# A hybrid decoder step on one core: the first expert step placed after the second group's combine, and the sample's attention on 128 rows

## The reference, cut to what matters

```
q, k, v, u = x @ w_in
a = diff_attention(q, k, v)          # 4 heads, two maps each: softmax0 - lam * softmax1, ALiBi, causal
s = s5_mixer(u)                      # state space branch
x = layer_norm(ALPHA * x + concat(a, s) @ w_out)
x = layer_norm(ALPHA * x + peer(x))

def diff_attention(...):             # sample: q 8 x 8 rows, k and v: 8 cached pages of 128 rows, and the 8 new rows
    s = einsum('bqhcd,bkhcd->bhcqk', q, k) * DQK ** -0.5
    s = where(causal, s - slope[h] * abs(dist), MASK)
    p = softmax(s)
    o = einsum('bhqk,bkhd->bqhd', p[:, :, 0] - lam * p[:, :, 1], v)
    return rms_norm(o, subln_g) * (1 - lam_init)

def peer(x):                         # 8 heads, 16 of 16384 single-neuron experts for each head and row
    q = rms_norm(x @ w_q)
    s_top, i_top = top_k(q @ sub_keys, 16)           # two halves of 128 keys
    best, pos = top_k(all 256 sums of a pair of halves, 16)
    g = softmax(best)
    act = gelu(einsum('thkd,td->thk', u_tab[idx], x))
    return einsum('thk,thkd->td', g * act, v_tab[idx])
```

## Time and profile before

| | us |
|---|---|
| median of 3 runs | 3920.2 |
| lowest, highest | 3915.3, 3923.3 |
| the profiled execution's own time | 3909.7 |
| its span, first to last instruction | 3907.1 |
| busy in the span: PE, DVE, ACT, POOL | 2720.8, 2430.5, 1499.2, 1285.4 |
| first gather, last gather issued at | 483.1, 3882.9 |
| mean granted clock of TensorE | 0.781 |

### The profile page before, as it was taken

How to read it: one execution, slowest core, us unless ns; L and a number is a source line. 1 busy time by engine, 2 the same in 40 slices (tenths; PEclk the granted TensorE clock), 3 DMA queues, 4 the chain that set the end, 5 groups by cost and what they waited for, 6 DMA issues and landing times.

```text
span 3907.1 us, 43487 instructions
## 1 busy us (share of the span) xinstructions
PE 2720.8 (70%) x13628; PEld 1104.0 (28%) x13628; DVE 2430.5 (62%) x5666; ACT 1499.2 (38%) x4347; POOL 1285.4 (33%) x1099
## 2 busy tenths in 40 slices
PE   7999475666676666666766776667666767787666
PEld 4677221122122212221232223123212332232221
DVE  8501486568557855775577558766876685334684
ACT  1111134434444444434443444344445444333343
POOL 0000034433443344344434442444344332112333
PEclk9999777786777678777877777678767877888866
DMA  6321499989999999899989998999899989767888
GB/s 140 82 81 57 152 404 398 413 333 384 402 379 371 371 405 369 360 382 417 375 341 395 410 370 339 397 410 379 343 397 411 372 342 378 268 253 302 326 341 344
DMA packets 240485, 1308.09 MB, mean 335 GB/s; under 512 B 41618, under 2 KB 69554, under 8 KB 90482
## 3 DMA queue, kind: packets, MB, share of 16 engines
q0 software_dynamic: 156672, 1140.92, 72.6%
q1 hardware_dynamic: 81890, 159.13, 11.8%
q10 hardware_dynamic: 1696, 5.27, 0.4%
HBM read 1285.65 MB, written 17.97 MB: 334 GB/s over the span
## 4 chain that ended last, share of the span: by engine, by line
DMA 30%; DVE 22%; PE 19%; ACT 8%; issue 7%; POOL 2%; SPq 2%; DVEq 0%; POOLq 0%
DMA UV<-in_peer_uv,icur 29%; DVE junk L1380 9%; PE psum L1045 9%; PE psum L971 3%; PE psum L991 3%; POOL UV L880 2%; PE psum L949 2%; ACT L1145 2%; ACT D L1150 1%; ACT wge L1147 1%; DMA wq<-in_cache_k 1%; DVE E L1340 1%; DVE sc L1287 1%; DVE E L1347 1%; ACT E L1056 1%
## 5 line engine op out<-in xcount | busy, mean ns | idle before, releaser
L1045 PE MATMUL psum<-UV,D 64*64 64x512 f32 x8704 | 1557.0, 810 | 1030.7 <-ACT D L1150 945.8
L880 POOL DMA_INDIRECT UV<-in_peer_uv,icur x1088 | 1279.8, 1176 | 2217.4 <-PE psum L1045 1788.7
L1380 DVE CUSTOM_DVE_ANT_0 junk<-UV,x 128x1024 bf16<-128x1024 f32 x1088 | 1333.7, 1226 | 862.1 <-DMA UV<-in_peer_uv,icur 791.9
L1145 ACT ACTIVATE ge<-acts 128x1 f32<-128x1 f32 x1088 | 219.7, 202 | 1774.0 <-DVE acts L1380 1772.9
L1045 PEld LDWEIGHTS psum<-UV,D 64*64 64x64 f32 x8704 | 321.7, 163 | 1953.3 <-issue 1860.6
L1150 ACT ACTIVATE D<-id,wge 128x64 f32<-128x64 f32 x1088 | 378.3, 348 | 35.4
L1147 ACT ACTIVATE wge<-ge,gcur 128x1 f32<-128x1 f32 x1088 | 320.5, 295 | 35.3
L991 PE MATMUL psum<-wq,aT 128*128 128x256 f32 (+1 forms) x1152 | 307.3, 426 | 1.2 <-ACT aT L1095 1.2
L991 PEld LDWEIGHTS psum<-wq,aT 128*128 128x128 f32 (+1 forms) x1152 | 235.2, 210 | 118.8 <-issue 72.4
L1145 ACT ACT_TABLE_LOAD x112 | 143.7, 1283 | 2.0
L308 PE MATMUL psum<-w_in_sb,xT 128*128 128x256 f32 (+1 forms) x576 | 129.6, 383 | 0.0
(11 more groups left out here) (295 smaller groups left out, 2415.4 us busy)
## 6 DMA issues: line engine op xcount, KB each, us to landing
wq<-in_peer_w_q SPq DMA_DIRECT2D x72, 1024.0 KB, 9.1
UV<-in_peer_uv,icur POOLq DMA_INDIRECT x1088, 10.1
wq<-in_cache_k SPq DMA_DIRECT2D x64, 256.0 KB, 7.1
vrows<-in_cache_v SPq DMA_DIRECT2D x64, 256.0 KB, 6.6
w_in_sb<-in_w_in SPq DMA_DIRECT2D x8, 1024.0 KB, 7.2
x<-in_x_all SPq DMA_DIRECT2D x9, 512.0 KB, 14.5
w_out_sb<-in_w_out SPq DMA_DIRECT2D x1, 4096.0 KB, 17.3
out<-x ACTq DMA_DIRECT2D x8, 512.0 KB, 7.1
```

Source lines behind the costliest of these rows:

```text
L880: pool.indirect_dma_start(out=UV[:, n % RING, :], out_offset=None, in_=table, in_offset=bass.IndirectOffsetOnAxis(ap=icur[:, t % 2, column ...
L1045: ins = pe.matmul(bank[6 + r][q:q + 64, :], D[64 * r:64 * r + 64, n % RING, :], UV[64 * r:64 * r + 64, n % RING, DM + 512 * e:DM + 512 * e ...
L1145: act.activation(ge[:, j:j + 1], acts[:, j:j + 1], ACT.Gelu).then_inc(sem("gelu_done"), 1)
L1380: dve.tensor_tensor_reduce(out=junk[:, :], in0=UV[:, n % RING, 0:DM], in1=x1[:, t % 2, :], scale=1.0, scalar=0.0, op0=ALU.mult, op1=ALU.ad ...
```

## The change

`lead(t)` is now five steps past the start of the combine of group 1 instead of group 0: 88 for a prompt tile and 96 for the sample tile. The first expert step of a tile so follows the second group's combine. Since index copies of several groups of the sample tile can now be under way before its first gather, the semaphore `spread` is split into one for each group.

The sample's attention uses 128 rows, 32 for each head (of which 16 are used: two maps of eight queries). A score matmul of a head writes its own 32 PSUM rows, with no adding over heads, and a value matmul of a head takes only this head's 128 columns of V. The map is transposed with all 128 rows, in two PSUM banks and two copies. The head mask `wm` goes; four scalings write the diagonal blocks of `Om`, a part of `E` that is set to zero once.

```diff
         def lead(t):
 
-            return combine_at(t, 0) + 5
+            return combine_at(t, 1) + 5
...
             if t == NT:
-                wait(pool, "spread", 16 + 32 * (g + 1))
+                wait(pool, f"spread{g}", 32 if g else 48)
...
                 for h in range(H):
-                    last = pe.matmul(bank[e][0:64, 0:n], qbd[:, h, :], kT[:, h, k0:k0 + n], start=h == 0, stop=h == H - 1)
+                    last = pe.matmul(bank[e][32 * h:32 * h + 32, 0:n], qbd[:, h, :], kT[:, h, k0:k0 + n], start=True, stop=True)
...
             for pg in range(PG):
-                pe.transpose(bank[0][:, 64 * pg:64 * pg + 64], Ef[0:64, P * pg:P * pg + P], ident[0:64, 0:64])
+                pe.transpose(bank[pg // 4][:, pg % 4 * P:(pg % 4 + 1) * P], Ef[:, P * pg:P * pg + P], ident[:, :])
...
             for pg in range(PG):
-                pe.matmul(bank[2][0:64, :], aT[:, pg, 0:64], vrows[:, pg, :], start=pg == 0, stop=False)
-            pe.matmul(bank[2][0:64, :], PTn[:, :], vnew, start=False, stop=True).then_inc(sem("s_O"), 1)
+                for h in range(H):
+                    pe.matmul(bank[2][32 * h:32 * h + 32, 0:DV], aT[:, pg, 32 * h:32 * h + 32], vrows[:, pg, h * DV:(h + 1) * DV],
+                              start=pg == 0, stop=False)
+            for h in range(H):
+                last = pe.matmul(bank[2][32 * h:32 * h + 32, 0:DV], PTn[:, 32 * h:32 * h + 32], vnew[:, h * DV:(h + 1) * DV],
+                                 start=False, stop=True)
+            last.then_inc(sem("s_O"), 1)
...
-                act.activation(aT[:, :, 0:64], bank[0][:, :].rearrange("p (g r) -> p g r", g=PG), ACT.Copy)
-                act.activation(PTn[:, :], bank[1][0:DS, 0:64], ACT.Copy).then_inc(sem("s_PT"), 1)
+                for e in range(2):
+                    act.activation(aT[:, 4 * e:4 * e + 4, :].rearrange("p g r -> p (g r)"), bank[e][:, :], ACT.Copy)
+                act.activation(PTn[:, :], bank[2][0:DS, 0:P], ACT.Copy).then_inc(sem("s_PT"), 1)
...
                 for c in range(2):
-                    for h in range(H):
-                        last = dve.tensor_copy(flat[64 * c:64 * c + 64, 80 * h + DS * c:80 * h + DS * c + DS],
-                                               qT[64 * c:64 * c + 64, h, DS * b:DS * b + DS])
+                    last = dve.tensor_copy(qbd[64 * c:64 * c + 64, :, DS * c:DS * c + DS],
+                                           qT[64 * c:64 * c + 64, :, DS * b:DS * b + DS])
...
                 wait(dve, "s_O", b)
-                dve.tensor_tensor(Ef[0:64, SEQ + 16:SEQ + 16 + DA].rearrange("p (h v) -> p h v", h=H),
-                                  bank[2][0:64, :].rearrange("p (h v) -> p h v", h=H),
-                                  wm[:, 0:H].rearrange("p (h u) -> p h u", u=1).broadcast_to((64, H, DV)), ALU.mult)\
-                   .then_inc(sem("s_Om"), 1)
+                for h in range(H):
+                    last = dve.tensor_scalar(Om[32 * h:32 * h + 32, h * DV:(h + 1) * DV], bank[2][32 * h:32 * h + 32, 0:DV],
+                                             small[32 * h:32 * h + 32, 6:7], None, ALU.mult)
+                last.then_inc(sem("s_Om"), 1)
```

More of the change, by code:

```diff
@@ L766, in trunk @@
         Ef = E[:, :]
+        Om = E[:, SEQ + 16:SEQ + 16 + DA]
         def S2(c, nk):
@@ L864, in sp_spread @@
                 wait(sp, "x1_ready", NT + 1)
-                sp.dma_start(x1[SR:P, NT % 2, :], x1[0:SR, NT % 2, :]).then_inc(sem("spread"), 16)
+                sp.dma_start(x1[SR:P, NT % 2, :], x1[0:SR, NT % 2, :]).then_inc(sem("spread0"), 16)
             p0, p1 = groups(NT)[g]
@@ L869, in sp_spread @@
                 pairs = cur[:, NT % 2, TOP * p0:TOP * p1].rearrange("p (q s k) -> p s q k", s=2, k=TOP)
-                sp.dma_start(pairs[SR:P, 0, :, :], pairs[0:SR, 1, :, :]).then_inc(sem("spread"), 16)
+                sp.dma_start(pairs[SR:P, 0, :, :], pairs[0:SR, 1, :, :]).then_inc(sem(f"spread{g}"), 16)
         def pool_gather(pool, t, k):
@@ L1188, in dve_sample_setup @@
             wait(dve, "aT_ps", 4 * NT)
-            step(dve.tensor_scalar(bias[0:64, 0:WB], bias[0:64, 0:WB], rowc[:, 6:7], None, ALU.add))
-            step(dve.tensor_scalar(bias[0:64, WB:SEQ], bias[0:64, WB - P:WB], float(P), None, ALU.add))
-            step(dve.tensor_scalar(bias[0:64, SEQ:], iot[0:64, 0:DS], rowc[:, 0:1], None, ALU.subtract))
-            step(dve.tensor_scalar(wm[:, 0:DS], bias[0:64, SEQ:], 0.0, MASKED, ALU.is_gt, ALU.mult))
-            step(dve.tensor_tensor(bias[0:64, SEQ:], bias[0:64, SEQ:], wm[:, 0:DS], ALU.add))
+            step(dve.tensor_scalar(bias[:, 0:WB], bias[:, 0:WB], rowc[:, 6:7], None, ALU.add))
+            step(dve.tensor_scalar(bias[:, WB:SEQ], bias[:, WB - P:WB], float(P), None, ALU.add))
+            step(dve.tensor_scalar(bias[:, SEQ:], iot[:, 0:DS], rowc[:, 0:1], None, ALU.subtract))
+            step(dve.tensor_scalar(wm[:, 0:DS], bias[:, SEQ:], 0.0, MASKED, ALU.is_gt, ALU.mult))
+            step(dve.tensor_tensor(bias[:, SEQ:], bias[:, SEQ:], wm[:, 0:DS], ALU.add))
+            step(dve.memset(Om, 0.0))
         def dve_sample(dve, step, b, r):
@@ L1501, in _ @@
                 q, slope, mw, hf, cf, rf = (rowc[:, n:n + 1] for n in range(6))
+                spare = rowc[:, 7:8]
                 step(dve.tensor_copy(rf, rowi[:, 0:1]))
-                for dst, sh, mask in ((q, 0, DS - 1), (cf, 3, 1), (hf, 4, H - 1)):
+                for dst, sh, mask in ((q, 0, DS - 1), (cf, 3, 1), (hf, 5, H - 1), (spare, 4, 1)):
                     step(dve.tensor_scalar(rowi[:, 1:2], rowi[:, 0:1], sh, mask, ALU.arith_shift_right, ALU.bitwise_and))
@@ L1508, in _ @@
                 step(dve.tensor_scalar(rowc[:, 6:7], rowc[:, 6:7], float(SEQ - P - PAST), None, ALU.add))
-                step(dve.tensor_scalar(mw, neglam[0:64, :], -1.0, None, ALU.add))
+                step(dve.tensor_scalar(mw, neglam[:, :], -1.0, None, ALU.add))
                 step(dve.tensor_scalar(mw, mw, cf, 1.0, ALU.mult, ALU.add))
-                step(dve.tensor_scalar(headm[:, :], iot[0:64, 0:H], hf, None, ALU.is_equal))
+                step(dve.tensor_scalar(headm[:, :], iot[:, 0:H], hf, None, ALU.is_equal))
                 step(dve.tensor_scalar(slope, headm[:, 0:1], SLOPE[0], None, ALU.mult))
@@ L1519, in _ @@
                 step(dve.memset(sel[:, :], 0.0))
-                step(dve.tensor_scalar(sel[:, 56:56 + DS], iot[0:64, 0:DS], q, None, ALU.is_equal))
+                step(dve.tensor_scalar(spare, spare, 64.0, None, ALU.mult))
+                step(dve.tensor_tensor(spare, spare, q, ALU.add))
+                step(dve.tensor_scalar(sel[:, 56:56 + DS], iot[:, 0:DS], spare, None, ALU.is_equal))
                 for f in range(lead(0)):
```

38 lines of the change are left out of this document (18 added, 20 removed).

## The result

| | before | after |
|---|---|---|
| median, us | 3921.3 (4 runs) | 3803.2 (4 runs) |
| lowest, highest | 3915.3, 3923.3 | 3797.1, 3809.7 |
| ratio, 95% interval | | 0.9701 [0.9682, 0.9721] |
| span of the profiled execution | 3907.1 | 3795.2 |

The change takes 118 us off, 109 to 125 by the interval. The forecast was 3800 us, 120 us less than before.

A forecast was written before the change was run, and what follows sets the result against it. DMA was taken as the bound, with time to win only where its engines are not full. Boundaries -77, last boundary -16, startup +7 and sample -34 make -120 us, giving 3800 us as likeliest, range 3760 to 3848.

The forecast's parts named there:

- The seven boundaries: Tile boundaries before the last: gathers no longer wait for group 0's combine, 11 of 12.9 us saved each, -77 us in all.
- VectorE's deficit: Around a tile boundary VectorE falls 6 us behind DMA; buffers cover most, not TensorE's stall for the sum; 2 us idle left.
- The last boundary: Boundary into the sample tile, where group 1 waits for its spread too: -16 us of 22.1, bounds -10 to -20.
- The start: Tile 0: nothing hides front steps 78 to 87, first dot near 501; +7 us, bounds +3 to +12.
- The sample: Sample's attention in tile 7: shorter values save 4.3 us a group, map costs 0.7, last scores save 5; -34 us in all.
- The map's dearer copies: Sample's attention: map transposed in 128 rows and copied by two ScalarE operations instead of one, +0.7 us in the chain.
- DMA moves the same bytes, gathers a little earlier: Sample's attention: the transferred bytes stay the same and gathers come slightly earlier; no time was assigned to this.
- The four heads' scalings: Sample's attention: four scalings of 128 replace one of 512; all VectorE edits cancel within 0.5 us, none in the loop.
- A: Sample's attention: column groups run one after another, values stay 9 to 10 us, sample costs 0 to +12; 3840 us, chance 0.14.
- B: Tile boundaries not freed: combine, sum and layer norm meet, 5 instead of 11 us saved at each of seven; 3842 us, chance 0.15.
- C: Sample's attention: each column-group change costs a drain, 0.28 us a record, deciding from about 0.16; 3988 us, chance 0.03.
- D: More gain than forecast: values run at full clock and all boundaries give 13, 14 us each; 3772 us, chance 0.08.

## Why the prediction was right, point by point

**The seven boundaries: right, the mechanism and the size.** The waits vanished as forecast and the DMA share went above 0.9. By the windows shown, 34 x 0.04 + 50 x 0.03 = 2.9 us of idle DMA remain at this boundary where 2 were left, so it gives 10; over all seven the idle time falls from 91 to 13.8 us, 11 each, where the forecast took 11. In clock time, at equal bytes, step 36 of tile 7 comes 2773.8 to 2778.1 us after the first gather in the four traces with the old lead (mean 2775) and 2699.1 to 2711.8 in the seven with the new one in all tiles (mean 2707): 68 us with the start in it, 10 for each boundary. The 1 us between the two readings was not traced. Read at step 26, where the changed kernel is 3.7 MB ahead, each boundary would seem to give 9 only. The argument that VectorE's deficit would leave TensorE's stall for the sum in place was wrong in kind: that stall fell from 83.8 to 25.4 us.

**The last boundary: mis-sized, 8 us instead of 16.** By the windows shown, 34 x 0.26 + 50 x 0.10 = 13.8 us stay idle where the forecast left 6 of 22.1, and that is below even its lower bound of 10. From step 98 of tile 7 to step 32 of the sample tile the kernel before takes 214.2 and 215.3 us, the changed one 198.5, and the nine others with its lead for the sample tile 196.7 to 199.7, which looks like the forecast 16. But about half of that is work moved out of the stretch: between steps 98 and 110 the kernel before has 7.6 us of idle DMA time and the changed one none, whose front steps stand earlier, and with the lead alone it is none either. What holds the DMA back at this boundary was not settled; the wait for the spread is gone (GpSimd's longest wait in the first window is 8.50 us, for a buffer), and VectorE is busy 31.26 of the 34 us.

**The start: the term mis-sized, 1 us instead of 7.** This is below the lower bound of 3. Its pieces were about right: the first dot follows the first gather after 20.9 us (18 was forecast), and the seventh gather follows after 26.0 us instead of 10.8 (23 was forecast). What was wrong is that the DMA time in between is lost for good. Of the first 160 us behind the first gather, cut into windows of 20 us, here are the second and the fifth of the changed kernel, and the second and the sixth of the kernel before:

```profile
509.00:529.00 20.00, 14.67 (x78) 6.35 (x78) 18.41 (x58) 8.66 (x32) 5.41 (x5) 0.73 0.88 315
...
569.00:589.00 20.00, 11.81 (x56) 2.54 (x56) 18.69 (x33) 12.26 (x30) 6.00 (x6) 0.52 0.90 338
```

```profile
503.00:523.00 20.00, 14.21 (x74) 7.01 (x74) 18.76 (x56) 11.19 (x26) 6.92 (x6) 0.76 1.01 419
...
583.00:603.00 20.00, 10.49 (x44) 1.67 (x40) 18.98 (x34) 10.12 (x23) 6.67 (x6) 0.50 0.93 364
```

The changed kernel loses 2.4 us in the second window. Over all 160 us the idle DMA time is 5.0 us against 4.2 and 4.5, because the query weights and inputs that the fronts load come in the gap (3.2 MB beside the gathers in the first 37 us, against 1.1) and don't compete with the gathers later. The lower bound's reason, that query weights fill it, was right, and the bound still too high. The kernel with the old lead in tile 0 shows the same 1 us.

**The sample: the sum about right, two of its pieces off in opposite directions.** The clean comparison is the kernel with this part alone, whose front steps stand where they stood: from step 26 to step 98 of tile 7 the kernel before takes 374.8 and 377.9 us and that one 340.8, 34 to 37 us for the forecast 34, and its time is 38 us less. In the changed kernel the six rounds have 20 us of idle DMA time less and the stretch behind them 8 less, 29 in all. Six rounds of 3.5 us are 21; the forecast counted eight of 3.6, and most of the rest of its sum came behind the last V issue. In the mean of these rounds, from V issue to K issue, to the first key transpose, to the values and to the next V issue, the kernel before needs 10.5, 10.9, 9.1 and 9.6 us, the changed one 10.6, 13.2, 9.5 and 3.1. The map's dearer copies cost 0.4 instead of 0.7. The values take 2.4 us where 5.0 were taken, so 2.6 more are saved. Half clock was the wrong assumption there, as the windows of the changed kernel show (columns as in the earlier trace rows): the clock is 0.53 while K is awaited, 0.93 from 3314 on, and 1.00 in the 2.3 us of the values.

```profile
3286.46:3311.00 24.54, 8.38 (x69) 2.46 (x67) 9.27 (x16) 5.07 (x16) 3.98 (x4) 0.74 0.97 364
...
3297.20:3314.00 16.80, 2.99 (x16) 1.88 (x16) 2.96 (x8) 2.41 (x6) 0.00 (x0) 0.53 0.86 336
3314.00:3323.60 9.60, 7.53 (x113) 4.93 (x105) 3.53 (x9) 7.25 (x16) 1.87 (x2) 0.93 0.50 153
```

Part of the gain came back as transfer time: K lands 2.3 us later after its issue (1.8 against the second trace of the kernel before). "DMA moves the same bytes, gathers a little earlier" was the step that left this out. In this round four gathers leave 2.1, 4.1, 7.1 and 9.2 us after the V issue, before 2.1, 4.1, 9.6 and 14.6, since the scores between them are short; so four gathers instead of three are ahead of K. From V issue to K landing the first of the windows above moves 24.54 us x 364 GB/s = 8.9 MB, the same stretch before 7.7 MB:

```profile
3391.93:3413.80 21.87, 13.78 (x69) 4.63 (x67) 8.81 (x20) 5.09 (x16) 4.18 (x4) 0.87 0.95 353
```

That more is moved ahead of K's landing is shown. That the order of the fourth gather and K is what counts is not: with doubled scores only three gathers are ahead in four of the six rounds, and K still needs 13.2 us. TensorE's wait for K was 14.3 us a sequence, above the 11 to 13 forecast. That the scores lie outside the loop is shown for this kernel by the doubled scores; for the kernel before it was only read from the trace, and it can hold only as long as the keys are late.

**The four heads' scalings** (L1228), which the forecast took to cancel against the other VectorE edits within 0.5 us, last 348 ns each (busy, mean ns | idle before), 1.4 us for four against 0.68 for the one. Nobody's wait is put down to them.

```profile
L1228 DVE TENSOR_SCALAR E<-psum,small 32x128 f32<-32x128 f32 x32 | 11.1, 348 | 34.5 <-PE psum L954 34.2
```

**The sum of it.** In idle DMA time: against the first and the second trace of the kernel before, start +1 and +0.5, seven boundaries -78 and -77, last boundary -8.5, sample -28 and -30, everything else -2.5 and -8, together -115.5 and -123. From the first gather to the last dot the clock has -118.5 and -124.8, and the medians -118 [-125, -109]. The two mis-sized terms of the lead, 6 us too dear and 8 us too cheap, cancel, and so do the two pieces of the sample; that the total came within 3 us of 3800 is in part luck.

**The rivals.** A fell: values take 2.4 us, and the kernel that forces their order into it is 49 us slower. B fell: the seven boundaries give 10 to 11 us each, not 5. C fell: a record that changes column group costs 1.95 / 64 = 0.03 us, far below the 0.16 from which it decides. D was right in one half, the values ran warm, and wrong in the other. The Trainium skill's caution ("TensorEngine Tiling (Array Packing)", Instruction Overhead), some 60 cycles for each matmul, read as the prediction read it, on top of the columns of every record, is not what this trace shows: by it the values would have been the 3.7 us or more that the prediction worked out beside its sum, and they took 2.4. The section's own example, that a matmul of one column lasts as long as one of sixty, reads rather as a floor, and records of 128 columns are above it. Nor do short records add up across groups: the eight score records of 8 columns add 0.04 us in four groups (1.11 against 1.07), where they added 0.42 in one (4.07 against 3.65).

## What to carry to other kernels

Price an earlier start by the DMA share in windows before and behind the gap, and take off what other transfers fill in. Compare two traces where the same bytes have moved, not at the same step, when the change moves work between steps. When one step in a loop gets shorter, read what it lets loose in the same queue or on the same engines, and look at once for the next bound: here the gain in the sample's attention went from some 35 us to some 90 only when the transfer that had become last was issued from where its buffer falls free rather than where program order had left it. Small matmuls in column groups pay when neighbours in the program go to different groups, so write the loop with the group innermost.

## What the runs showed of the hardware

- 64 records of 128 columns in four column groups took 1.95 us with neighbours in different groups. With only the order changed, 16 records of one group took 1.94 us, 0.12 each, and the four groups followed one another. The granted clock was 1.00 in both.
- At four groups side by side a record of 128 columns costs 0.03 us in all. In one column group it costs 0.12 us. In the kernel before, eight score records of 512 columns took 3.65 us, 0.46 each, at a granted clock of 1.00 as well; a quarter of that is 0.11. By these two, an estimate: a record costs about a hundredth of a us beyond its columns.
- TensorE's busy time in the sample's loop fell from 31 to 19 us a round. It is the layout: with the old lead and the new layout one round has 19.6 us.
